# A wider stride between the stationary activation tiles of a one-core decoder layer

## The reference

```
h   = x + token_mixing(rmsnorm(x))          # x: (256, 4096)
  token_mixing(xn):
    proj   = xn @ w_in                      # 4096 -> 5200 columns, and z = xn @ gate_down (256 columns)
    o_i    = four attention branches on proj
    merged = sum_i sigmoid(z @ gate_up[i]) * (o_i @ w_branch[i])
    return merged @ w_out                   # 4096 x 4096
out = h + peer_ffn(rmsnorm(h))
  peer_ffn(xn):
    q    = xn @ wq                          # 4096 x 1024
    pick 16 of 64 x 64 experts for each of 8 heads
    act  = gelu(xn @ u.T)                   # 4096 x 4096
    wmat = gates scattered at the picked experts, times act
    return wmat @ v                         # 4096 x 4096
```

## Time and profile before

| | |
|---|---|
| median of three runs | 1932.3 us (1931.75 to 1932.71) |
| span of the profiled execution, first to last instruction | 1929.5 us |
| the profiled execution's own time | not given; median less span is 2.8 us |
| instructions | 26523 |
| TensorE matmuls / weight loads | 9254 / 9254 |
| granted TensorE clock, mean of the core | 1.000 |

### The profile page before, as it was taken

How to read it: one execution, slowest core, us unless ns; L and a number is a source line. 1 busy time by engine, 2 the same in 40 slices (tenths; PEclk the granted TensorE clock), 3 DMA queues, 4 the chain that set the end, 5 groups by cost and what they waited for, 6 DMA issues and landing times.

```text
span 1929.5 us, 26523 instructions
## 1 busy us (share of the span) xinstructions
PE 1925.1 (100%) x9254; PEld 1588.8 (82%) x9254; DVE 1274.6 (66%) x1876; ACT 934.1 (48%) x1146; POOL 37.0 (2%) x50
## 2 busy tenths in 40 slices
PE   9999999999999999999999999999999999999999
PEld 8888888888888888888888888888887788888887
DVE  6578775675557889655555555788878876444444
ACT  7653644444566556444444464444444454333332
POOL 0010010000000000000000000000000000000000
PEclk9999999999999999999999999999999999999999
DMA  9976566565655569877777776677776678666664
GB/s 328 344 221 164 167 176 197 165 163 167 188 177 176 182 201 297 281 228 245 231 244 217 215 224 227 227 214 215 221 215 187 176 228 289 202 205 206 201 204 140
DMA packets 198537, 412.62 MB, mean 214 GB/s; under 512 B 45760, under 2 KB 123968, under 8 KB 197792
## 3 DMA queue, kind: packets, MB, share of 16 engines
q1 hardware_dynamic: 173616, 368.83, 63.3%
q10 hardware_dynamic: 20976, 25.19, 3.9%
q0 software_dynamic: 3840, 17.17, 2.4%
HBM read 390.15 MB, written 20.97 MB: 213 GB/s over the span
## 4 chain that ended last, share of the span: by engine, by line
PE 100%; DVE 0%; issue 0%
PE acc L559 29%; PE acc L562 29%; PE acc L566 29%; PE acc L607 3%; PE acc L609 3%; PE acc L613 3%; PE side L735 1%; PE side L845 1%; PE acc L578 1%; PE acc L582 1%; PE acc L586 1%; PE side L770 0%; PE side L662 0%; PE side L746 0%; PE side L593 0%; PE side L700 0%
## 5 line engine op out<-in xcount | busy, mean ns | idle before, releaser
L1337 DVE TENSOR_TENSOR w_lo<-w_raw,w_hi 128x1024 fp32r<-128x1024 f32 (+1 forms) x680 | 825.5, 1216 | 607.1 <-ACT w_hi L976 604.4
L976 ACT ACTIVATE w_hi<-w_raw 128x1024 fp32r<-128x1024 f32 (+1 forms) x680 | 714.9, 1053 | 818.5 <-PE acc L566 747.3
L559 PE MATMUL acc<-w_hi,xt_hi 128*128 128x512 f32 x1660 | 449.0, 392 | 0.0
L562 PE MATMUL acc<-w_hi,xt_lo 128*128 128x512 f32 x1660 | 444.1, 389 | 0.0
L566 PE MATMUL acc<-w_lo,xt_hi 128*128 128x512 f32 x1660 | 443.9, 389 | 0.0
L562 PEld LDWEIGHTS acc<-w_hi,xt_lo 128*128 128x128 f32 x1660 | 311.6, 188 | 65.5
L566 PEld LDWEIGHTS acc<-w_lo,xt_hi 128*128 128x128 f32 x1660 | 311.6, 188 | 65.1
L559 PEld LDWEIGHTS acc<-w_hi,xt_hi 128*128 128x128 f32 x1660 | 308.7, 188 | 63.7 <-issue 1.4
L559 PE MATMUL acc<-w_hi,x_hi 128*128 128x512 f32 x640 | 175.0, 395 | 0.0
L562 PE MATMUL acc<-w_hi,x_lo 128*128 128x512 f32 x640 | 171.8, 390 | 0.0
L566 PE MATMUL acc<-w_lo,x_hi 128*128 128x512 f32 x640 | 171.2, 389 | 0.0
(11 more groups left out here) (277 smaller groups left out, 1348.1 us busy)
## 6 DMA issues: line engine op xcount, KB each, us to landing
w_raw<-in_stream SPq DMA_DIRECT2D x504, 512.0 KB, 4.3
w_raw<-in_w_in SPq DMA_DIRECT2D x16, 496.0 KB, 4.0
w_raw<-in_w_in SPq DMA_DIRECT2D x16, 480.0 KB, 4.3
w_raw<-in_w_in SPq DMA_DIRECT2D x16, 464.0 KB, 3.8
w_raw<-in_w_in SPq DMA_DIRECT2D x16, 448.0 KB, 3.7
w_raw<-in_w_in SPq DMA_DIRECT2D x16, 432.0 KB, 4.0
w_raw<-in_w_in SPq DMA_DIRECT2D x16, 416.0 KB, 4.0
w_raw<-in_w_in SPq DMA_DIRECT2D x16, 400.0 KB, 3.7
```

Of the source, the lines that this page charges most:

```text
L559: pe.matmul(o[h], lhs(k0 + j, h)[0], wh[j], start=first and j == 0, stop=False)
L562: pe.matmul(o[h], lhs(k0 + j, h)[1], wh[j], start=False, stop=False)
L976: nc.scalar.activation(w_hi[:, slot, 0:width], w_raw[:, slot, 0:width], ACT.Copy).then_inc(hi_ready, 1)
L1337: nc.vector.tensor_tensor(w_lo[:, slot, 0:width], w_raw[:, slot, 0:width], w_hi[:, slot, 0:width].bitcast(F32), ALU.subtract).then_inc(lo_ ...
```

## The change

The tiles of `xt_hi` are declared with 4 more elements each and used without them, so tile k begins at 1040 k bytes instead of 1024 k. That makes the tensor 512 bytes longer, so `xt_lo`, the tensors that lie in its place and the regions RG0, MG0 and CN0 all move up by 512 bytes. To find the room, `cmp_h` and `row_at` go into unused elements of `small`, and `iota_h` is placed at the end without rounding up. The two flat operations on pairs of `xt_hi` tiles get a two-dimensional pattern, as the pairs are no longer one run.

```diff
-    RG0 = XT0 + 64 * KB
+    RG0 = XT0 + 64 * KB + 512
...
-    xt_hi = at("xt_hi", [P, KT, S], F32R, XT0)
-    xt_lo = at("xt_lo", [P, KT, S], F32R, XT0 + 32 * KB)
+    xt_hi = at("xt_hi", [P, KT, S + 4], F32R, XT0)[:, :, 0:S]
+    xt_lo = at("xt_lo", [P, KT, S], F32R, XT0 + 32 * KB + 512)
...
-    cmp_h = const("cmp_h", [P, 2, NCMP])
...
-    x3_hi = at("x3_hi", [P, KT - NX2, S], F32R, XT0 + 40 * KB)
-    x3_lo = at("x3_lo", [P, KT - NX2, S], F32R, XT0 + 48 * KB)
+    x3_hi = at("x3_hi", [P, KT - NX2, S], F32R, XT0 + 40 * KB + 512)
+    x3_lo = at("x3_lo", [P, KT - NX2, S], F32R, XT0 + 48 * KB + 512)
...
-    row_at = const("row_at", [P, PK])
...
-    iota_h = const("iota_h", [P, P], BF16)
+    iota_h = at("iota_h", [P, P], BF16, cursor[0])
...
-    act_t = at("act_t", [P, KT // 2, 4, 2, NT, 32], F32, XT0)
+    act_t = at("act_t", [P, KT // 2, 4, 2, NT, 32], F32, XT0 + 512)
...
+    row_at = piece(PK)
+    cmp_h = piece(2 * NCMP).rearrange("p (w n) -> p w n", n=NCMP)
...
-                nc.scalar.activation(flat(xt_hi[:, 2 * q:2 * q + 2, :]), flat(wmat[:, 2 * q:2 * q + 2, :]), ACT.Copy)\
+                nc.scalar.activation(xt_hi[:, 2 * q:2 * q + 2, :], wmat[:, 2 * q:2 * q + 2, :], ACT.Copy)\
...
-                nc.vector.tensor_tensor(flat(xt_lo[:, 2 * q:2 * q + 2, :]), flat(wmat[:, 2 * q:2 * q + 2, :]),
-                                        flat(xt_hi[:, 2 * q:2 * q + 2, :]).bitcast(F32), ALU.subtract)\
+                nc.vector.tensor_tensor(xt_lo[:, 2 * q:2 * q + 2, :], wmat[:, 2 * q:2 * q + 2, :],
+                                        xt_hi[:, 2 * q:2 * q + 2, :].bitcast(F32), ALU.subtract)\
```

More of the change, by code:

```diff
@@ L299, in build @@
     subkeys = at("subkeys", [P, PH, P], F32, XT0 + 16 * KB)
-    act_t = at("act_t", [P, KT // 2, 4, 2, NT, 32], F32, XT0)
+    act_t = at("act_t", [P, KT // 2, 4, 2, NT, 32], F32, XT0 + 512)
     key_s = at("key_s", [P, NT, PH, 2, 64], F32, XT0 + 32 * KB)
-    act_rows = at("act_rows", [P, 4, 4, NT, 32], F32, XT0 + 56 * KB)
-    act_blk = at("act_blk", [P, 4, 256], F32, XT0 + 60 * KB)
+    act_rows = at("act_rows", [P, 4, 4, NT, 32], F32, XT0 + 56 * KB + 512)
+    act_blk = at("act_blk", [P, 4, 256], F32, XT0 + 60 * KB + 512)
     act_d = nc.dram_tensor("act_blocks", (4, 32, 4, 256), F32, kind="Internal").ap()
@@ L315, in build @@
     hot_1 = at("hot_1", [P, HOT, 32], BF16, T0 + 10 * KB)
-    hot_c = [at(f"hot_c{i}", [P, HOT, P], BF16, XT0 + (32 + 2 * i) * KB) for i in range(3)]
-    gate_r = at("gate_r", [P, 2, S], F32, XT0 + 38 * KB)
+    hot_c = [at(f"hot_c{i}", [P, HOT, P], BF16, XT0 + (32 + 2 * i) * KB + 512) for i in range(3)]
+    gate_r = at("gate_r", [P, 2, S], F32, XT0 + 38 * KB + 512)
     look = at("look", [P, UNITS, PK, PK], F32, XT0 + 28 * KB)
```

## The result

The kernel after takes 1955.42 us (median of four runs, 1955.22 to 1955.47) against 1932.35 us for the kernel before on the same chip: a ratio of 1.012, with a 95% interval of 1.0107 to 1.0132. It is 23.1 us slower. The forecast was no change, and the range, 1905 to 1938 us, missed it.

What follows compares the result with a forecast made beforehand. The prediction took TensorE's matmul pace to bound the kernel. All terms summed to 0 on the path against the profiled 1929.5 us; adding 2.8 us to reach the median gave 1932.3 us, with a range of 1905 to 1938 us.

Steps and rivals of the forecast that it cites:

- What bounds the kernel: Whole span: TensorE's matmul pace at full clock, 226.7 ns per 512 columns, 13.3 ns beyond the columns; suppliers are ahead.
- I take 0, as the nearest rows are the fp32r ones, where 512, 1024 and 1344 bytes make no difference at all.: Stride of xt_hi, loads for L559 and L566: priced 0, between 46.1 us gained and 34.6 us lost.
- Against: the gap is exactly the same in every stage: Argument against an address collision: same 13.3 ns in every stage, three regions, both widths; a collision should show some exception.
- The count: Loads from xt_hi for L559 and L566 that the stride touches: 3448 recorded, 3456 by the code.
- The slower rival: L559 and L566, tiles with k not a multiple of 4: gap grows 1.7 ns, 4.3 us lost, 1936.6 us; chance 0.14.
- Its upper bound: Gap doubled for three of four xt_hi tiles: 2592 x 13.3 = 34.6 us lost, 1966.9 us.
- The faster rival: xt_hi matmuls: gap is a collision the stride breaks; half freed gains 23.0 us, 1909.3 us, all freed 1886.2; chance 0.26.
- The 512-byte move, the patterns and the small tensors: Regions moved 512 bytes, two-dimensional patterns at L1235 and L1843, cmp_h, row_at and iota_h relocated: each 0 on the path.
- the load's spare time: xt_hi weight loads: a slower load would be hidden, with over 110 ns spare in the 226.7 ns period.

Runs made afterwards that it cites:

- the scan: TensorE alone, none of the layer computed, 120 matmuls a placement; at 336 columns, tile steps of 1024 and 1040 bytes took 153.4 and 154.1 ns per matmul.

## Why the prediction was wrong, point by point

**What bounds the kernel** was right, and so was where the time had to be looked for: 13.3 ns beyond the columns of each fp32r matmul. Alone, plain float32 with its 429.2 ns stands 2.5 ns over twice 213.3, and bf16 with its 215.9 stands 2.6 ns over 213.3. One reading was incomplete: besides the 13 us for streamed weights ScalarE waited 17.5 us for those of w_in, which changes nothing, as TensorE fills the span.

**"I take 0, as the nearest rows are the fp32r ones, where 512, 1024 and 1344 bytes make no difference at all."** This step failed: a term that no row could price was put at nothing, between 46.1 us gained and 34.6 us lost. It was 4.9 ns on each of 4992 matmuls, 24 us by the stretches, 23.1 us in the medians. The rows were no witnesses: 512 and 1024 are multiples of 256, so all of them were one placement. The one that wasn't, 1344, came from matmuls of 336 columns, and the scan shows that those hardly feel the change's own step, 0.7 ns against 4.8 with 512 columns. Rows that all lie at one point of the unknown variable bound nothing, however many they are.

**"Against: the gap is exactly the same in every stage"** was read the wrong way round. An exact 2720 ns in every chunk doesn't show that addresses don't matter; it shows that all stages had the same distance. Tiles 32 bytes later ran just as exactly, at 2800 ns.

**The count** of matmuls was wrong as well: I priced the 3456 loads from xt_hi. The 1660 recorded matmuls on xt_lo lost 6.2 of the 22.9 us. It fits this that a rhythm broken at one tile isn't back at the next; no run here shows it apart.

**The slower rival** had the right side and, of the three lines, two, but the wrong price and the wrong cause: an eighth of the gap on 2592 loads, 4.3 us, for tiles off a multiple of 64. All tiles 16 bytes later ran at 226.66 ns alone, and the ring moved by 128 cost 29 us with no tile moved. Its upper bound, 34.6 us, would have held the result, but partly by luck: the slow rhythm, 233.3 ns, is only half a gap above the fast one, and it strikes 4992 matmuls instead of 2592. (These 2592 are half of all products of the three stages, not the two thirds that the prediction says.) The range stopped at 1938, just above the rival's 1936.6, and left out most of the way to that bound, 1966.9.

**The faster rival** is refuted for this step, and none of the placements tried loses the gap. The sentence of the Trainium skill (TensorE: Matmul & The Clock Gate, Part 2, step 1), that loading the next tile takes no read bandwidth from the running matmul, doesn't fit fp32r here: the same loads beside the same matmuls cost 13.3 or 20 ns by address. The traces don't show by what path the two streams meet, nor that it is read bandwidth that is lost.

**The 512-byte move, the patterns and the small tensors** at 0 were right (1932.05 us), as was "the load's spare time": the recorded load stayed at 188 ns. That spare time did not help, because the matmuls became slower and not the load.

Open is the mechanism inside, for no run shows the two streams themselves: what lies at 256 bytes, why there are rhythms of 2720 and 2800 ns (544 and 560 cycles of 2.4 GHz a matmul), and what holds under 32 bytes.

## What to carry to other kernels

In a kernel bound by fp32r matmuls, keep the start of every stationary tile and of every moving tile at the same place modulo 256 bytes, and keep it so when a region is moved (both operands 32, 64 or 128 bytes later settled at the fast pace, both 16 later did not, 231.1 ns): 512 bytes cost nothing here, 128 bytes 29 us, a pad of 16 bytes a tile 23 us. Read an even pace as a sign that all tiles share one placement, not that placement is free. A scan of placements on the bound engine alone costs one run and would have priced this change beforehand: 4.8 ns on 4992 matmuls, 24 us for 23.1. All this was seen with a load before each matmul and 512 columns.

## What the runs showed of the hardware that was not expected

- An fp32r matmul of 512 columns with a fresh load each time takes 226.66 ns at best and 233.3 ns at most bad distances (234.2 at the worst); bf16 takes 216 ns and plain float32 429.2 ns, at a step of 1024 and of 1040 bytes.
- One placement can have two stable paces, 226.7 and 232.7 ns, and side work of less than 2 us moves the kernel from one to the other for many chunks.
- With 336 columns the step of 1040 costs 0.7 ns, with 512 columns 4.8.
